# Masks added by VectorE with the maximum, and compressions' first layer in plain fp32 on four column groups

## The chip, the cores and the metric

One of the eight cores of a Trainium2 chip runs the kernel. The metric is the device time in microseconds, from the kernel's start to its end; lower is better.

## The reference

The kernel computes two transformer blocks over 256 tokens of width 1024, in fp32. The first has a gated feed-forward, a mixing stage (NSA attention with compressed, selected and windowed keys, next to sliding-window attention with sinks) and a second feed-forward. The second block has two layers, each with a mixing stage of three kinds (MLA, DSA with a top-k selection, retention) and a feed-forward. What the change touches is this:

```python
def _compress(kv, pe, w1, w2):                    # 15 blocks of 32 tokens, 2 groups
    blocks = jnp.concatenate([c[:, :-1], c[:, 1:]], axis=2)
    blocks = blocks + pe[None, None, :, None, :]
    flat = blocks.transpose(0, 1, 3, 2, 4).reshape(B, n_cmp, G, CMP_LEN * D)
    return jax.nn.gelu(flat @ w1) @ w2            # w1: 2048 x 256, w2: 256 x 64

s = jnp.einsum('bnqgrd,bnkgd->bngrqk', qb, kb) * (D ** -0.5)
s = jnp.where(mask[None, :, None, None], s, NEG_INF)
m = jnp.maximum(jnp.max(s, axis=-1, keepdims=True), sk)     # sk: the sinks, swa only
e = jnp.exp(s - m)
p = e / (jnp.sum(e, axis=-1, keepdims=True) + jnp.exp(sk - m))
```

Every attention (slc, win, swa in the first block, dsa and mla in the second) masks its scores, subtracts the row's maximum and takes the exponential. dsa's mask is computed at run time from the top-k selection, the others are constant.

## The kernel before

**Order.** One list, `schedule()` (L128), holds the steps of the whole program. Each engine walks the same list and issues its part of every step, so the list sets the order on every engine, and each engine works strictly in order. Semaphores join them.

**Weights.** Weights come in pieces ("slabs") of 1 MB, in a ring of three buffers `raw`. SP loads piece s when piece s - 3 no longer needs its buffer (L746). Precision is kept by splitting: ScalarE copies a piece to `w_hi` rounded (the high half, L998), VectorE writes the rest, raw minus high, to `w_lo` (the low half, L1357), and TensorE then makes three matmuls for each product: high times high, high times low, low times high (`group`, L1873). On ScalarE and VectorE `ahead` (L1005, L1365) issues the splits up to two pieces ahead of the step, before that step's own work. TensorE waits for the low half.

**Compressions.** Step `xpe` adds the position embeddings on VectorE (L1670, into `xpe`, 16 blocks of 30 columns), and both halves of the result are made (L1241, L1673). Step `cmp1` takes two pieces, of 8 blocks each: per block three matmuls with 30 stationary and 256 moving columns (L2149), all into one bank. ScalarE applies Gelu (L1247), TensorE turns the result (`cmpt`, L2158), ScalarE copies it, TensorE does the second layer (`cmp2`).

**Attention.** A "tile" is 128 queries: t = 0 has 128 keys, t = 1 has 256. Heads are handled in groups that fill one bank of 512 columns: four heads for t = 0, two for t = 1 (`groups`, L177; dsa has two in both). Two groups make a round: they sit on different halves of TensorE's rows, and their matmuls alternate (mla's groups stand alone). Per round:

- `s` on TensorE: a bf16 matmul of the identity with the mask starts the bank (L2199), then the plain fp32 score matmuls add to it (L2204). VectorE reduces the bank to the negative maximum of each head (L1687), ScalarE takes the exponential from the bank with that as bias, one head at a time, with the sum (L1285), and that frees the bank.
- `t`: TensorE turns the probabilities (L2212), VectorE copies them (L1702; dsa's ScalarE, L1294).
- `pv`: TensorE multiplies with the values (L2226).

In the first block nine rounds, slc 0, slc 1 (two), win 0, win 1 (two), swa 0, swa 1 (two), are interleaved with eight gate projections ("gate", one piece each, g0 to g7), so that a round's `t` comes one round after its `s`, and its `pv` one more after that. In the second block mla's and dsa's steps stand with fewer projections between them.

**Rope.** A projection is copied by ScalarE to `xs` (L1218), multiplied by a constant matrix on TensorE (L2138), and combined by VectorE in two passes (L1648, L1657), with a product from GpSimd (L972). A matmul in plain fp32 leaves two records in the trace.

## Time and profile before

| | |
|---|---|
| three runs, us | 1279.13, 1282.40, 1281.95; median 1281.95 |
| profiled execution, span | 1277.6 us (the time around its span isn't given) |
| TensorE busy | 1252.2 us (98%), 8858 matmul records |
| VectorE busy | 810.5 us (63%) |
| ScalarE busy | 613.4 us (48%) |
| GpSimd busy | 86.5 us (7%) |
| DMA | 209.94 MB, mean 164 GB/s |
| granted TensorE clock | full speed in all 40 slices |

The span is what the hardware profiler saw of one execution, from the first to the last instruction. A duration of a matmul contains the time that it takes to pass through the array, and overlaps the next one's: what a matmul costs is the distance from its start to the start of the next. PE is TensorE, PEld its weight loads, DVE VectorE, ACT ScalarE, POOL GpSimd, SP the engine that issues loads.

### The profile page before, as it was taken

The numbers are of one execution on the slowest core, as the hardware profiler recorded it, in microseconds if no ns is written. First come the engines' busy times: TensorE is split into PE (matmuls) and PEld (weight loads), VectorE is DVE, ScalarE is ACT, GpSimd is POOL, SyncE is SP. The second block draws the span as 40 slices with busy tenths as digits, with TensorE's granted clock in tenths as the row PEclk, the third lists the DMA queues.
The fourth block names the chain that finished last, engine by engine and source line by source line (L and its number), as shares of the span: only waits on it lengthen the run. The fifth ranks groups of instructions, "written<-read, shape, count | busy, mean of one in ns | idle before, by whom it ended". The sixth has DMA issues, their size and how long they took to land. (4 is left out here: it accounts for less than half of the span.)

```text
span 1277.6 us, 21605 instructions
## 1 busy us (share of the span) xinstructions
PE 1252.2 (98%) x8858; PEld 1151.6 (90%) x8858; DVE 810.5 (63%) x965; ACT 613.4 (48%) x836; POOL 86.5 (7%) x73
## 2 busy tenths in 40 slices
PE   8999999999999999999999999999999999999997
PEld 7999999989898999999998889999999978999996
DVE  5665556676866655556798756555459976655554
ACT  5443436473436443435744554444465364544443
POOL 0000001100000000001432000000014210000000
PEclk9999999999999999999999999999999999999999
DMA  9565666463236565556535056655644334565560
GB/s 284 191 208 195 195 161 165 156 199 101 98 108 206 178 194 188 190 175 187 166 108 165 16 179 201 196 177 187 189 134 149 91 131 148 166 197 175 187 197 33
DMA packets 181461, 209.94 MB, mean 164 GB/s; under 512 B 32537, under 2 KB 158097, under 8 KB 181265
## 3 DMA queue, kind: packets, MB, share of 16 engines
q1 hardware_dynamic: 180944, 208.52, 52.3%
q8 instruction: 49, 0.80, 0.3%
q10 hardware_dynamic: 448, 0.46, 0.1%
q14 instruction: 20, 0.16, 0.0%
HBM read 207.92 MB, written 1.05 MB: 164 GB/s over the span
## 5 line engine op out<-in xcount | busy, mean ns | idle before, releaser
L1357 DVE TENSOR_TENSOR w_lo<-raw,w_hi 128x2048 fp32r<-128x2048 f32 (+2 forms) x198 | 441.7, 2234 | 271.1 <-ACT w_hi L998 270.7
L998 ACT ACTIVATE w_hi<-raw 128x2048 fp32r<-128x2048 f32 (+2 forms) x198 | 367.8, 1861 | 234.6 <-PE bank L1879 215.6
L1879 PE MATMUL bank<-n_hi,w_hi 128*128 128x256 f32 (+1 forms) x1600 | 455.5, 285 | 1.2 <-DVE w_lo L1357 1.2
L1879 PE MATMUL bank<-n_hi,w_lo 128*128 128x256 f32 (+1 forms) x1600 | 452.5, 283 | 0.0
L1879 PE MATMUL bank<-n_lo,w_hi 128*128 128x256 f32 (+1 forms) x1600 | 452.5, 283 | 0.0
L1879 PEld LDWEIGHTS bank<-n_hi,w_hi 128*128 128x128 f32 (+1 forms) x1600 | 305.1, 191 | 5.1 <-DVE w_lo L1357 2.1
L1879 PEld LDWEIGHTS bank<-n_lo,w_hi 128*128 128x128 f32 (+1 forms) x1600 | 305.2, 191 | 2.3 <-issue 0.5
L1879 PEld LDWEIGHTS bank<-n_hi,w_lo 128*128 128x128 f32 (+1 forms) x1600 | 305.1, 191 | 0.0
L1879 PE MATMUL bank<-w_hi,hid_hi 128*128 128x512 f32 (+1 forms) x472 | 182.3, 386 | 1.3 <-DVE hid_lo L1430 1.1
L1879 PE MATMUL bank<-w_lo,hid_hi 128*128 128x512 f32 (+1 forms) x472 | 180.6, 383 | 0.0
L1879 PE MATMUL bank<-w_hi,hid_lo 128*128 128x512 f32 (+1 forms) x472 | 180.2, 382 | 0.0
L1879 PEld LDWEIGHTS bank<-w_hi,hid_hi 128*128 128x128 f32 (+1 forms) x472 | 86.2, 183 | 19.4 <-issue 2.5
L1879 PEld LDWEIGHTS bank<-w_hi,hid_lo 128*128 128x128 f32 (+1 forms) x472 | 86.0, 182 | 18.0
L1879 PEld LDWEIGHTS bank<-w_lo,hid_hi 128*128 128x128 f32 (+1 forms) x472 | 86.2, 183 | 16.1 <-issue 0.6
L1015 ACT ACTIVATE scr<-scr 128x512 f32<-128x512 f32 x22 | 13.9, 633 | 95.4 <-DVE scr L1412 95.4
L1879 PE MATMUL bank<-hid_hi,w_hi 128*96 128x256 f32 (+1 forms) x176 | 50.8, 289 | 2.4 <-issue 1.5
L1285 ACT ACTIVATE probs<-bank,negm 128x128 f32<-128x128 f32 (+1 forms) x96 | 39.0, 427 | 23.1 <-DVE negm L1687 23.1
L1879 PE MATMUL bank<-hid_lo,w_hi 128*96 128x256 f32 (+1 forms) x176 | 49.5, 281 | 0.0
L1879 PE MATMUL bank<-hid_hi,w_lo 128*96 128x256 f32 (+1 forms) x176 | 49.5, 281 | 0.0
L1426 DVE SCALAR_TENSOR_TENSOR scr<-bank,rstd 128x512 f32<-128x512 f32 x32 | 22.1, 691 | 42.2 <-PE bank L1879 42.1
L1956 PE MATMUL bank<-n_hi,w_hi 128*128 128x256 f32 x144 | 42.2, 293 | 3.3 <-DVE n_lo L1400 1.8
L1019 ACT ACTIVATE hid_hi<-scr 128x512 fp32r<-128x512 f32 x22 | 13.9, 630 | 59.2 <-DVE scr L1420 59.2
(259 smaller groups left out, 1527.6 us busy)
## 6 DMA issues: line engine op xcount, KB each, us to landing
raw<-in_w_ff_dram SPq DMA_DIRECT2D x64, 1024.0 KB, 5.3
raw<-in_w_in_dram SPq DMA_DIRECT2D x31, 1024.0 KB, 5.4
raw<-in_ffn_down_dram SPq DMA_DIRECT2D x22, 1024.0 KB, 5.0
raw<-in_ffn_up_dram SPq DMA_DIRECT2D x21, 1024.0 KB, 5.3
raw<-in_ffn_gate_dram SPq DMA_DIRECT2D x20, 1024.0 KB, 5.4
raw<-in_w_out_dram SPq DMA_DIRECT2D x12, 1024.0 KB, 5.2
raw<-in_w_uq_dram SPq DMA_DIRECT2D x8, 576.0 KB, 4.1
raw<-in_w_in_dram SPq DMA_DIRECT2D x12, 256.0 KB, 4.0
```

The costliest lines, as they stand in the source:

```text
L998: nc.scalar.activation(w_hi[:, s % SPLIT, c0:n], raw[:, s % RING, c0:n], ACT.Copy).then_inc(hi_ready, 1)
L1015: nc.scalar.activation(silu_sb, silu_sb, ACT.Silu).then_inc(silu_ready, 1)
L1019: nc.scalar.activation(hid_hi[:, buf, :], hid[:, buf, :], ACT.Copy).then_inc(hidh_ready, 1)
L1285: last = nc.scalar.activation(probs[:, buf, c], pb[:, c], ACT.Exp, bias=negm[:, buf, i:i + 1], accum_out=rsum[:, RSLOT[a], t, h:h + 1])
L1357: V.tensor_tensor(w_lo[:, s % SPLIT, c0:n], raw[:, s % RING, c0:n], w_hi[:, s % SPLIT, c0:n].bitcast(f32), ALU.subtract).then_inc(lo_ready, 1)
L1426: V.scalar_tensor_tensor(halves(silu_sb), halves(bank[b][:, :]), 0.0, r2(), ALU.max, ALU.mult).then_inc(bank_free[b], 1)
L1879: mm = MM(out, stat(k, a), mov(k, b), start=(first and k == 0 and n == 0), stop=(last and k == K - 1 and n == 2), skip_group_check=True)
L1956: mm = MM(pb[:, m * T:m * T + T], w(s, a)[:, k * T + m * P:k * T + m * P + P], xn(k, b), start=(k == 0 and m == 0 and j == 0), stop=(k == ...
```

## The change

Three parts.

1. **Masks.** The mask matmuls go. VectorE's step `s` becomes, for each head, one `tensor_tensor_reduce`: it adds score and mask, negates, writes the result to `probs` in SBUF and reduces it to the minimum (the negative maximum). Each is two instructions, the pass and a read of the accumulator. VectorE's last pass frees the bank, ScalarE's exponential reads `probs` with scale -1 and writes it in place. Since VectorE now writes `probs`, it is VectorE that waits for the transposes of four groups before.
2. **Compressions.** The four pieces of `cmp1` (k and v, two halves each) are not split; TensorE reads `raw`. Per block one plain fp32 matmul, 32 stationary columns (`xpe` is padded), block i to the column group i mod 4, which is partitions 32(i mod 4) and on of the bank. Step `cmpt` is a matmul with a constant `fold` that turns and adds the four groups in one; Gelu moves behind it. The buffer of such a piece is free when TensorE has multiplied it (`slab_done`), where it was when VectorE had split it.
3. **Order.** In `schedule()` slc 1 comes before slc 0 (its first round needs only the rope of nq0), cmp1 of k stands before the first scores, projection sq1 and the rope of nq1 between the first and the second round of scores, cmp1 of v after gate 1.

```diff
@@ schedule @@
           ("rope", 0, "nq0"), ("proj", 0, "vv"), ("rope", 0, "sk"), ("proj", 0, "sq0"), ("rope", 0, "k"),
-          ("xpe", "k"), ("proj", 0, "nq1"), ("rope", 0, "sq0"), ("xpe", "v"), ("proj", 0, "sq1")]
-    scores, turned, weighted = in_rounds(0, [(a, t) for a in ("slc", "win", "swa") for t in range(NT)])
+          ("xpe", "k"), ("proj", 0, "nq1"), ("rope", 0, "sq0"), ("xpe", "v"), ("cmp1", "k")]
+    scores, turned, weighted = in_rounds(0, [("slc", 1), ("slc", 0)] + [(a, t) for a in ("win", "swa") for t in range(NT)])
-    S += [("rope", 0, "nq1"), ("cmp1", "k")] + scores[0] + [("rope", 0, "sq1"), ("cmp1", "v")] + scores[1] + turned[0]
-    S += gate[0] + [("cmpt", "k")] + scores[2] + weighted[0] + turned[1]
-    S += gate[1] + [("cmp2", "k"), ("cmpt", "v")] + scores[3] + weighted[1] + turned[2]
-    S += gate[2] + [("cmp2", "v"), ("rope", 0, "kc")] + scores[4] + weighted[2] + turned[3]
-    S += gate[3] + [("cs", 0)] + scores[5] + weighted[3] + turned[4]
+    S += scores[0] + [("proj", 0, "sq1"), ("rope", 0, "nq1"), ("cmpt", "k")] + scores[1] + [("rope", 0, "sq1")] + turned[0]
+    S += gate[0] + [("cmp2", "k")] + scores[2] + weighted[0] + turned[1]
+    S += gate[1] + [("cmp1", "v"), ("rope", 0, "kc")] + scores[3] + weighted[1] + turned[2]
+    S += gate[2] + [("cmpt", "v")] + scores[4] + weighted[2] + turned[3]
+    S += gate[3] + [("cmp2", "v"), ("cs", 0)] + scores[5] + weighted[3] + turned[4]
@@ load_slab @@
-            if s >= RING:
-                sp.wait_ge(lo_ready, s - RING + 1)
+            if s >= RING and slabs[s - RING][0] == "cmp1":
+                sp.wait_ge(slab_done, s - RING + 1)
+            elif s >= RING:
+                sp.wait_ge(lo_ready, LOC[s - RING])
@@ ScalarE @@
                 elif kind == "cmp1":
                     ahead(SL[st + (0,)])
                     ahead(SL[st + (1,)])
                     pb = await_bank(act, st)
-                    nc.scalar.activation(cmp_h[:, v, :], pb[0:2 * NCMP, 0:T], ACT.Gelu_apprx_tanh).then_inc(freed(st), 1)
+                    nc.scalar.activation(cmp_h[:, v, :], pb[:, 0:T], ACT.Copy).then_inc(freed(st), 1)
...
-                    act.wait_ge(negm_ready, q + 1)
-                    if q >= 4:
-                        await_bank(act, ("t",) + ATTLIST[q - 4])
+                    act.wait_ge(*free_count(st))
...
-                        last = nc.scalar.activation(probs[:, buf, c], pb[:, c], ACT.Exp, bias=negm[:, buf, i:i + 1],
+                        last = nc.scalar.activation(probs[:, buf, c], probs[:, buf, c], ACT.Exp, bias=negm[:, buf, i:i + 1], scale=-1.0,
                                                     accum_out=rsum[:, RSLOT[a], t, h:h + 1])
-                    last.then_inc(freed(st), 1)
+                    last.then_inc(exp_done, 1)
@@ VectorE @@
-                    ins = V.tensor_reduce(negm[:, buf, 0:nh], pb[:, 0:nh * nk].rearrange("p (h k) -> p h k", h=nh), AX.X, ALU.max, negate=True)
+                    if q >= 4:
+                        await_bank(dve, ("t",) + ATTLIST[q - 4])
+                    if a == "dsa":
+                        dve.wait_ge(retv_done, l)
+                        dve.wait_ge(sel_ready, 2 * (l - 1) + t + 1)
+                    for i in range(nh):
+                        c = slice(i * nk, i * nk + nk)
+                        ins = V.tensor_tensor_reduce(out=probs[:, buf, c], in0=pb[:, c], in1=mask_of(a, t), scale=-1.0, scalar=3e38,
+                                                     op0=ALU.add, op1=ALU.min, accum_out=negm[:, buf, i:i + 1])
+                    ins.then_inc(freed(st), 1)
@@ TensorE @@
-                    pe.wait_ge(xpel_ready, v + 1)
+                    pe.wait_ge(xpe_ready, v + 1)
                     for half in range(2):
                         s = SL[st + (half,)]
-                        weights(s)
+                        pe.wait_ge(raw_ready[s % RING], RAWC[s])
                         for i in range(8):
-                            c = (8 * half + i) * 30
-                            mm = group(pb[0:2 * NCMP, 0:256], 1, lambda k, lo: (xpe_lo if lo else xpe_hi)[:, v, c:c + 30],
-                                       lambda k, lo: w(s, lo)[:, i * 256:i * 256 + 256], first=(half == 0 and i == 0),
-                                       last=(half == 1 and i == 7))
+                            r = slice(32 * (i % 4), 32 * (i % 4) + 32)
+                            mm = MM(pb[r, 0:256], xpe[v][:, 256 * half + 32 * i:256 * half + 32 * i + 32], raw[:, s % RING, i * 256:i * 256 + 256],
+                                    start=(half == 0 and i < 4), stop=(half == 1 and i >= 4), skip_group_check=True)
                         mm.then_inc(slab_done, 1)
...
-                        mm = nc.tensor.transpose(pb[:, m * P:m * P + 2 * NCMP], cmp_h[:, v, m * P:m * P + P], ident[0:2 * NCMP, 0:2 * NCMP])
+                        mm = MM(pb[:, m * P:m * P + 32], cmp_h[:, v, m * P:m * P + P], con("fold"), start=True, stop=True, skip_group_check=True)
...
-                    for pb, heads, _ in sides:
-                        nh = len(heads)
-                        part = pb[:, 0:nh * nk].rearrange("p (h k) -> p h k", h=nh)
-                        m = mask_of(a, t)
-                        if a in ("slc", "win", "mla"):
-                            part, m = part[:, :, t * P:t * P + P], m[:, t * P:t * P + P]
-                        MM(part, identb[:, :], m.unsqueeze(1).to_broadcast([P, nh, m.shape[1]]), start=True, stop=False, skip_group_check=True)
```

**Where instructions move.** First VectorE between the rope of k and that of nq1. `work` is the compressions' input, `turn_s` and the `scr` beside it are a rope's two passes, `w_lo` a low half, `negm` the negative maxima. Before (the rope of nq1 is the pair in the middle):

```order
L1670 TENSOR_TENSOR work<-work,gains 128x8x15 x3
L1673 TENSOR_TENSOR hid_lo<-work,hid_hi 128x480 [waits xpeh_ready]
L1357 TENSOR_TENSOR w_lo<-raw,w_hi 128x2048 [waits hi_ready]
L1648 TENSOR_TENSOR turn_s<-bank,rvt 128x512 [waits rope_done,tab_ready,bank_ready1]
L1657 TENSOR_TENSOR scr<-turn_c,turn_s 128x512 [waits turnc_ready,bank_free1]
L1357 TENSOR_TENSOR w_lo<-raw,w_hi 128x2048 [waits hi_ready] x2
L1687 TENSOR_REDUCE negm<-bank 128x4 [waits bank_ready7]
L1687 TENSOR_REDUCE negm<-bank 128x4 [waits bank_ready4]
```

After the change (the rope of sq0, the v blocks, the low halves of sq1 and g0, the first round, the low half of g1, the rope of nq1):

```order
L1652 TENSOR_TENSOR turn_s<-bank,rvt 128x512 [waits rope_done,tab_ready,bank_ready0]
L1661 TENSOR_TENSOR scr<-turn_c,turn_s 128x512 [waits turnc_ready,bank_free0]
L1671 MEMSET work 128x32 [waits xpe_ready]
L1675 TENSOR_TENSOR work<-work,gains 128x8x15 x4
L1361 TENSOR_TENSOR w_lo<-raw,w_hi 128x2048 [waits hi_ready] x2
L1697 ISA probs,negm<-bank,masks 128x256 [waits bank_ready6]
L1697 ISA negm 128x1
...
L1361 TENSOR_TENSOR w_lo<-raw,w_hi 128x2048 [waits hi_ready]
L1652 TENSOR_TENSOR turn_s<-bank,rvt 128x512 [waits rope_done,tab_ready,bank_ready5]
L1661 TENSOR_TENSOR scr<-turn_c,turn_s 128x512 [waits turnc_ready,bank_free5]
```

The rope of nq1, which stood ahead of the first maxima, now stands behind the first round and behind the low half of g1.

Second ScalarE around the compression of k: `w_hi` is a high half, `xs` a projection's copy. Before:

```order
L1218 ACTIVATE xs<-bank 128x512 [waits slab_done,rope_done]
L998 ACTIVATE w_hi<-raw 128x2048 [waits slab_done,raw_ready1]
L998 ACTIVATE w_hi<-raw 128x2048 [waits slab_done,raw_ready2]
L1247 ACT_TABLE_LOAD
L1247 ACTIVATE rgt<-bank 30x256 [waits slab_done]
L1285 ACT_TABLE_LOAD
L1285 ACTIVATE probs,rsum<-bank,negm 128x128 [waits negm_ready]
```

Now (the high halves are those of sq1, g0 and g1; the last `xs` is sq1's):

```order
L1228 ACTIVATE xs<-bank 128x512 [waits slab_done,rope_done] x2
L1008 ACTIVATE w_hi<-raw 128x2048 [waits slab_done,raw_ready0]
L1008 ACTIVATE w_hi<-raw 128x2048 [waits slab_done,raw_ready1]
L1253 ACTIVATE rgt<-bank 128x256 [waits slab_done]
L1287 ACT_TABLE_LOAD
L1287 ACTIVATE probs,rsum<-probs,negm 128x256 [waits bank_free6]
...
L1008 ACTIVATE w_hi<-raw 128x2048 [waits slab_done,raw_ready2]
L1228 ACTIVATE xs<-bank 128x512 [waits slab_done,rope_done]
```

The high half of g1 and the copy of sq1 now stand behind the first round's exponentials.

Third ScalarE around the compression of v. Before, with the high halves of two gate pieces ahead of Gelu:

```order
L998 ACTIVATE w_hi<-raw 128x2048 [waits slab_done,raw_ready0]
L998 ACTIVATE w_hi<-raw 128x2048 [waits slab_done,raw_ready1]
L1247 ACT_TABLE_LOAD
L1247 ACTIVATE rgt<-bank 30x256 [waits slab_done]
L1285 ACT_TABLE_LOAD
```

Now, with those of g2 and g3 ahead of the copy that frees the compression's bank:

```order
L1287 ACTIVATE probs,rsum<-probs,negm 128x128 [waits bank_free5]
L1287 ACTIVATE probs,rsum<-probs,negm 128x128 x3
L1008 ACTIVATE w_hi<-raw 128x2048 [waits slab_done,raw_ready2]
L1008 ACTIVATE w_hi<-raw 128x2048 [waits slab_done,raw_ready0]
L1253 ACTIVATE rgt<-bank 128x256 [waits slab_done]
```

g3 shares its `raw` buffer with the first half of v, and so its load waits for TensorE there.

## Rows read from the trace of the kernel before

**Rows 1.** The page's first part: busy time, share, instructions.

```profile
PE 1252.2 (98%) x8858; PEld 1151.6 (90%) x8858; DVE 810.5 (63%) x965; ACT 613.4 (48%) x836; POOL 86.5 (7%) x73
```

**Rows 2.** Windows: stretch, length, busy us of each engine (instructions), clock, DMA, GB/s.

```profile
247.05:357.64 110.59, 110.02 (x915) 100.39 (x913) 82.55 (x127) 61.28 (x144) 5.45 (x3) 1.00 0.43 134
695.40:711.00 15.60, 12.96 (x84) 10.13 (x83) 14.37 (x24) 12.29 (x27) 3.10 (x2) 1.00 0.18 68
```

**Rows 3.** TensorE's timeline, 246 to 261 us: start, us, engine, line, operation, count.

```profile
246.59 1.02 PE L2138 MATMUL bank<-xs,cst 128*128 128x512 f32 x2
247.05 0.68 PE L1879 MATMUL bank<-n_hi,w_hi 128*128 128x256 f32 x1
...
253.66 0.68 PE L1879 MATMUL bank<-w_hi,hid_hi 128*30 128x256 f32 x1
...
259.60 0.60 PE L2199 MATMUL bank<-masks,identb 128*128 128x512 bf16 x2
260.13 1.16 PE L2204 MATMUL bank<-scr 64*128 64x128 f32 x16
```

**Rows 4.** TensorE's timeline at the second round of scores.

```profile
267.73 0.39 PE L2199 MATMUL bank<-masks,identb 128*128 128x256 bf16 x2
268.06 1.13 PE L2204 MATMUL bank<-scr 64*128 64x256 f32 x8
```

**Rows 5.** The mask matmuls' line, and TensorE's timeline at mla's first scores.

```profile
L2199 PE MATMUL bank<-masks,identb x30: 269/283/389, 259.6 to 1056.6; 128*128 128x256 bf16 x16, 128*128 128x512 bf16 x14
L2199 PE MATMUL bank<-selb,identb x8: 273/330/377, 694.4 to 1033.7; 128*128 128x256 bf16 x4, 128*128 128x512 bf16 x4
...
709.53 0.38 PE L2199 MATMUL bank<-masks,identb 128*128 128x512 bf16 x1
709.75 1.06 PE L2204 MATMUL bank<-scr 96*128 96x128 f32 x8
...
711.75 0.28 PE L2199 MATMUL bank<-masks,identb 128*128 128x256 bf16 x1
711.87 1.03 PE L2204 MATMUL bank<-scr 96*128 96x256 f32 x4
712.73 0.27 PE L2199 MATMUL bank<-masks,identb 128*128 128x256 bf16 x1
```

**Rows 6.** TensorE's timeline: index scores on four row groups.

```profile
641.92 1.15 PE L2260 MATMUL bank<-scr 32*128 32x256 f32 x16
642.99 0.38 PE L1879 MATMUL bank<-n_hi,w_hi 128*128 128x256 f32 x1
```

**Rows 7.** The page's groups for the low and the high half; a load's landing.

```profile
L1357 DVE TENSOR_TENSOR w_lo<-raw,w_hi 128x2048 fp32r<-128x2048 f32 (+2 forms) x198 | 441.7, 2234 | 271.1 <-ACT w_hi L998 270.7
L998 ACT ACTIVATE w_hi<-raw 128x2048 fp32r<-128x2048 f32 (+2 forms) x198 | 367.8, 1861 | 234.6 <-PE bank L1879 215.6
...
DMA to landing us min/median/max: 3.9/5.2/10.6
```

**Rows 8.** VectorE's and ScalarE's timelines, 250 to 274 us.

```profile
250.26 1.17 DVE L1670 TENSOR_TENSOR work<-work,gains 128x120 f32<-128x120 f32 x4
...
262.23 1.28 DVE L1687 TENSOR_REDUCE negm<-bank 128x4 f32<-128x512 f32 x2
...
272.82 0.47 ACT L1285 ACTIVATE probs<-bank,negm 128x256 f32<-128x256 f32 x1 [0.38 <-DVE negm L1687]
273.19 0.19 ACT L1285 ACTIVATION_READ_ACCUMULATOR probs<-bank,negm 128x1 f32 x1
273.29 0.47 ACT L1285 ACTIVATE probs<-bank,negm 128x256 f32<-128x256 f32 x1
```

**Rows 9.** Timelines in the second block's first layer: dsa's and mla's first reductions, TensorE's longest wait.

```profile
695.49 0.76 DVE L1687 TENSOR_REDUCE negm<-bank 128x2 f32<-128x256 f32 x2 [0.32 <-PE bank L2204]
...
703.26 1.07 PE L2138 MATMUL bank<-xs,cst 96*96 96x512 f32 x2 [2.18 <-ACT probs L1285]
...
710.84 0.69 DVE L1687 TENSOR_REDUCE negm<-bank 128x4 f32<-128x512 f32 x1 [0.44 <-PE bank L2204]
```

More of the change, by code:

```diff
@@ L102, in constants @@
     put("blk", (rows[:, None] // CP == np.arange(8)[None, :]).astype(np.float32))
+    put("fold", (rows[:, None] % 32 == np.arange(32)[None, :]).astype(np.float32))
     q, k = np.arange(P)[:, None], np.arange(P)[None, :]
@@ L332, in two_blocks @@
         x2 = wflat[:, 0:1024].rearrange("p (v g t) -> p v g t", v=2, g=2)[:, :, :, :]
-        xpe = wflat[:, 1024:1024 + 480]
+        xpe = [wflat[:, at:at + 512] for at in (1024, 0)]
         vblk = wflat[:, 1536:2048]
@@ L620, in two_blocks @@
         ATTLIST = sorted(ATT, key=ATT.get)
+        SINKS = {st: n + 1 for n, st in enumerate(st for st in ATTLIST if st[1] == "swa")}
         IDX = [(t, [j, j + 4]) for t in range(NT) for j in range(4)]
@@ L1273, in _ @@
                     buf = q % 4
-                    act.wait_ge(negm_ready, q + 1)
-                    if q >= 4:
-                        await_bank(act, ("t",) + ATTLIST[q - 4])
-                    if a == "dsa":
-                        act.wait_ge(retv_done, l)
-                    pb = bank[JOB[st][0]]
+                    act.wait_ge(*free_count(st))
                     if a == "swa":
+                        act.wait_ge(sink_seen, SINKS[st[1:]])
                         hs = slice(heads[0], heads[-1] + 1, 2)
@@ L1669, in _ @@
                             src = x2[:, v, g, 16 * a:16 * a + 240].rearrange("p (c b e) -> p b c e", b=8, e=2)[:, :, :, 0]
-                            last = V.tensor_tensor(out_v[:, a, :, g, :], src, bc(gains[:, pe0 + 8 * a:pe0 + 8 * a + 8], 8, NCMP), ALU.add)
+                            last = V.tensor_tensor(out_v[:, a, :, g, 0:NCMP], src, bc(gains[:, pe0 + 8 * a:pe0 + 8 * a + 8], 8, NCMP), ALU.add)
                     last.then_inc(xpe_ready, 1)
-                    dve.wait_ge(xpeh_ready, v + 1)
-                    V.tensor_tensor(xpe_lo[:, v, :], xpe, xpe_hi[:, v, :].bitcast(f32), ALU.subtract).then_inc(xpel_ready, 1)
                 elif kind == "cmp1":
@@ L2187, in _ @@
                             pe.wait_ge(*free_count(("ukv", l, 1)))
-                        if a == "dsa":
-                            pe.wait_ge(sel_ready, 2 * (l - 1) + t + 1)
                     if a == "mla":
```

66 lines of the change are left out of this document (36 added, 30 removed).

## The prediction

> **What bounds the kernel now.** I read the page first: TensorE is busy 1252.2 of 1277.6 us [rows 1]. Then the windows: in the stretch that the change reorders, 247.05 to 357.64 us, TensorE is busy 110.02 of 110.59 us at a granted clock of 1.00, while VectorE is busy 82.55 and ScalarE 61.28 [rows 2]. So there every matmul removed is worth its time, unless the shortened work uncovers a wait. Third, the timeline for the price of each piece. A matmul's duration overlaps the next one's, so prices are differences of starts. Last, VectorE's timeline in the second block, where it is busy 14.37 of 15.60 us [rows 2]: there it has no room for new work. The profiled execution's own time is not given; its span of 1277.6 lies 4.35 us under the median of the three runs, 1281.95, so I forecast a difference and add it to the median.
>
> **Masks, on TensorE.** 38 mask matmuls go [rows 5]. In the first block a pair over 512 columns costs 260.13 - 259.60 = 0.53 us [rows 3], one over 256 columns 268.06 - 267.73 = 0.33 [rows 4]. There are five wide pairs (slc 0, win 0, swa 0 and both rounds of swa 1) and four narrow ones (both rounds of slc 1 and of win 1): 2.65 + 4 x 0.31 to 0.33, so 3.9. In each layer of the second block: a narrow and a wide pair for dsa (0.85), two wide single ones at 0.22 and four narrow ones at 0.12 for mla (0.92) [rows 5], 1.75 together.
>
> **Compressions' first layer.** Each takes 48 matmuls from 253.66 to 259.60, 5.94 us [rows 3]. Now it is 16 plain fp32 ones with 256 moving columns. A plain one of that shape costs (712.73 - 711.87) / 2 = 0.43 us: in mla four records, two matmuls, stood in 0.86 (the record at 711.87 runs 1.03 with its tail) [rows 5]. One after the other, 16 cost 6.9. Eight such matmuls on four row groups took 642.99 - 641.92 = 1.07 us [rows 6], two deep instead of eight: 0.87 and 0.2 for filling. No row shows column groups. If they overlap as row groups do, four deep is 1.74 + 0.2 = 1.94; ends 1.7 and 6.9, and I take 1.94, since the nearest row is idx. Saved: 2 x 4.0 = 8.0. The Trainium skill (TensorE: Matmul & The Clock Gate, section "Why this matters for your kernels") has column groups within a few ns of row groups, at 2.38x for three tiles; by that ratio a compression would take 2.9 us. Fold, memset and the wider constants cost under 0.2 us and lie beside other work.
>
> **VectorE's new price.** A group's maximum was one reduction, 0.60 us apart (two in 1.28) [rows 8]. Now each head has a masked minimum and a separate read of the accumulator: 96 of each. The split of 2048 columns takes 2.23, which is (2.23 - 0.68) / 1536 = 1.0 ns a column beyond the reduction's 512 [rows 7, 8]; so 0.60 is 0.52 of streaming and 0.08 of overhead, and a pass over 256 columns lies between 0.34 (pipelined) and 0.42 (its whole duration, 0.68 less 0.26). The read lies between 0 and the 0.19 that ScalarE's takes [rows 8]. I take 0.45 a head, close to the pipelined end, as reductions are pipelined; ends 0.34 and 0.61. For 128 columns: 0.32, ends 0.21 and 0.48. Four heads of 256 take 1.8 instead of 1.2, eight of 128 take 2.6.
>
> **Waits uncovered in the first block.** The short compression no longer covers the weights' pipeline. I take a load as 5.2 us to landing, ScalarE's high half as 1.9 and VectorE's low half as 2.2 us [rows 7]. By hand, from 247.05, where the compression of k now starts:
> 1. It ends at 249.0, the first scores at 250.1. The next projection, sq1, needs its low half, and VectorE has that behind rope sq0 (starts about 247.7, two passes, to 249.4) and the v blocks (four adds, 1.17 [rows 8], and a memset, to 250.8): ready 253.1. **TensorE waits 3.0.** It projects until 259.3 (6.15: 6.61 from 247.05 to 253.66 less a rope's 0.46 [rows 3]), then rope nq1 and the fold, to 260.3.
> 2. Gate piece g0 can be loaded only when the first half of k is multiplied, 248.2: landed 253.5, high 255.4, low 257.7. Only then come the masked minima (259.4), ScalarE's exponentials (0.45 apart [rows 8], to 260.4), the high half of g1 (262.3), its low half (264.6), and behind that on VectorE rope nq1, two passes (266.0). The second round of scores needs rope nq1: **TensorE waits 5.7.** No transposes stand between to fill it.
> 3. The same at v. There ScalarE's split of g3 stands ahead of the copy that frees the compression's bank, and gate 2 wants that bank. g3 is loaded after half of v: 5.2 + 1.9 + 0.4 + 0.1 of semaphores = 7.6 us; TensorE has 4.8 of other work (the second half, rope kc, scores, values, transposes). **2.8.** ScalarE is late by that for the next exponentials and g4, and gate 3's bank is freed behind g4's low half: **1.3.**
> Sum 12.8 of waits against 3.9 + 8.0 = 11.9 saved: +0.9 us. Later rounds keep VectorE under the round: the fullest has about 9.5 us of work and gains 0.6, against 10.5.
>
> **Second block.** VectorE is in one chain from 695.49 to the first mla reduction at 710.84 [rows 9], with only 0.44 of idle at its end. dsa's heads add 0.5 + 0.6, less 0.32 because its scores end earlier: first mla minimum about 0.3 us later and 0.6 longer. TensorE, 1.75 ahead, and 1.3 more from the wait of 2.18 before rope uq2 [rows 9] (bank 4 is now freed by VectorE, not by the exponentials), then stands at the scores of mla's second group, whose rope uq3 is in that chain. The rest of mla follows the exponentials. I find the end of mla 0.3 us later than before, in each layer: the masks' 1.75 is lost there. Ends of the price: 0.3 earlier, and 2.5 later. Total: 0.9 + 2 x 0.3 = **+1.5 us**, 1283.5.
>
> **Rivals.**
> - *The saving holds more than I find.* If the minima cost the pipelined end, and loads land a microsecond sooner (once at k, once at v), the waits lose 2 to 3 us, and where the second block's chain has slack its masks' 3.5 are kept: 0.9 - 2.5 - 3.5 = -5, 1277. For: VectorE idles 0.44 before mla. Against: it is a single in-order queue, and three costs must err the same way.
> - *The clock falls in the new wait.* Before, TensorE idles at most 2.18 us at once behind the start [rows 9], and the granted clock is 1.00 [rows 2]; the new wait of 5.7 has no like there. At 1.2 GHz, the scores, rope and transposes behind it (2.4 us) and part of a gate projection of 5.84 cost as much again: about +3, so 1286.5. It decides once a wait is long enough, which no row shows. The Trainium skill (TensorE: Matmul & The Clock Gate, "What's actually happening") says the array falls to half its clock when idle and needs sustained work to rise; by that rule the gap would be charged.
> - *The minima are dear.* At 0.61 and 0.48 the second block ends 2.5 later per layer and the k wait is 0.6 longer: +6, 1288. It decides from about 0.5 a head. For: two instructions per head; against: reductions overlap.
> - *The groups don't run together*, so that this part doesn't do what it says: 6.9 instead of 1.94 each. Of the 5.0 added at k half is absorbed (waits 1 shrinks), and so at v: first halves end 2.5 later, +5, so 1288.5. Against: row groups overlap [rows 6].
>
> **How the numbers follow.** About 0.3% (3.8 us) is what a measurement can tell from no change. Forecast 0.40 (its own range 1279 to 1286), first rival 0.25, clock 0.17, dear minima 0.10, serial groups 0.08. Faster takes 0.20 of the first rival and 0.05 of the forecast's lower edge; slower takes the last three (0.35 less the mild half of the clock's, 0.05) and 0.05 of the upper edge; the rest, 0.40, is the same. The range that leaves out two in ten is 1275 to 1290: from the first rival with a further 2 us to the serial case and its bounds.
>
> **What would show it.** Right: two gaps on TensorE near 250 to 253 and 260 to 266, released by the low half of sq1 and by VectorE's rope nq1; one of 2 to 3 us before gate 2, released by ScalarE's copy; compressions of 2 us; in 695 to 726 a VectorE without idle time and an end of mla at the same distance from its start as before. Wrong: a dense TensorE between 247 and 350 (then the change is worth some 10 us), compressions of 6 us or more, a granted clock under 1 behind 266, or a masked minimum of half a microsecond or more.

## The result, and the profile after

| kernel | median of 8 runs, us | ratio to the kernel before, 95% interval |
|---|---|---|
| before | 1281.38 (1279.13 to 1282.40) | |
| the change | 1284.88 (1283.74 to 1285.88) | 1.0031 [1.0021, 1.0042] |

The change makes the kernel slower by 3.5 us: measurable, and at the edge of the 0.3% that the prediction had taken as the least that can be told. The span of the profiled execution went from 1277.6 to 1282.2, 4.6 us more. That is more than the medians say because the profiled execution of the kernel before is one of its shortest: an execution of it with a span of 1277.5 took 1279.3, 2.1 under the median, and the change's profiled one took 1284.29, 0.6 under its own. The page's first part, beside [rows 1]:

```profile
PE 1242.6 (97%) x8792; PEld 1142.6 (89%) x8792; DVE 804.9 (63%) x1115; ACT 609.0 (48%) x831; POOL 85.6 (7%) x73
```

TensorE is busy 9.6 us less than before, and the span is 4.6 us longer: 14 us of new idle time. The page can't say where it lies. The windows can, where those of [rows 2] stood. The first mixing stage is now 116.62 us long, with a granted clock of 0.97. This window begins with the rotation of sq0, which stood just ahead of that of [rows 2]; counted from there too (246.59), the stage took 111.05 before, so it is 5.6 longer.

```profile
247.00:363.62 116.62, 102.83 (x870) 93.08 (x869) 77.96 (x202) 60.42 (x142) 4.46 (x3) 0.97 0.43 136
```

So in this stage TensorE idles 13.8 us. Its waits there (line waited for and what released it; total, times, longest):

```profile
PE bank L2207 <- DVE scr L1661: 7.2, 1, 7.2
PE bank L1890 <- ACT rgt L1253: 2.9, 1, 2.9
PE bank L1890 <- DVE w_lo L1361: 2.2, 1, 2.2
PE bank L1890 <- DVE scr L1630: 1.2, 1, 1.2
```

A fifth is 0.2, 13.7 in all. Before, the same stage had 0.6 us of waits, both short ones before scores. TensorE's timeline at the first two waits, beside [rows 3, 4]:

```profile
247.00 1.02 PE L2149 MATMUL bank<-xs,cst 128*128 128x512 f32 x2
247.95 1.93 PE L2160 MATMUL bank<-raw,work 128*32 128x256 f32 x32
249.81 1.13 PE L2207 MATMUL bank<-scr 64*128 64x256 f32 x8
253.11 0.39 PE L1890 MATMUL bank<-n_hi,w_hi 128*128 128x256 f32 x1 [2.16 <-DVE w_lo L1361]
...
259.83 0.54 PE L2168 MATMUL bank<-cst,rgt 128*128 128x32 f32 x4
267.58 2.08 PE L2207 MATMUL bank<-scr 64*128 64x256 f32 x8 [7.21 <-DVE scr L1661]
269.59 2.07 PE L2149 MATMUL bank<-xs,cst 128*128 128x512 f32 x2
271.46 1.35 PE L2215 MATMUL bank<-cst,probs 128*128 128x128 f32 x8
272.56 0.36 PE L1890 MATMUL bank<-n_hi,w_hi 128*128 128x256 f32 x1
```

The compression takes 1.86 us (247.95 to 249.81): the column groups do run together. Then come both gaps that the prediction named. What TensorE waits for in the second is VectorE's rotation of nq1, and VectorE's timeline shows what stands ahead of it:

```profile
250.78 2.27 DVE L1361 TENSOR_TENSOR w_lo<-raw,w_hi 128x2048 fp32r<-128x2048 f32 x1
256.64 2.29 DVE L1361 TENSOR_TENSOR w_lo<-raw,w_hi 128x2048 fp32r<-128x2048 f32 x1 [3.59 <-ACT w_hi L1008]
258.85 0.42 DVE L1697 CUSTOM_DVE_ANT_0 probs<-bank,masks 128x256 f32<-128x256 f32 x1
259.19 0.08 DVE L1697 DVE_READ_ACCUMULATOR2_ANT negm<- 128x1 f32 x1
259.19 0.42 DVE L1697 CUSTOM_DVE_ANT_0 probs<-bank,masks 128x256 f32<-128x256 f32 x1
...
263.56 2.29 DVE L1361 TENSOR_TENSOR w_lo<-raw,w_hi 128x2048 fp32r<-128x2048 f32 x1 [3.25 <-ACT w_hi L1008]
265.77 0.68 DVE L1652 TENSOR_TENSOR turn_s<-bank,rvt 128x512 f32<-128x512 f32 x1
266.49 1.04 DVE L1661 TENSOR_TENSOR scr<-turn_c,turn_s 128x512 f32<-128x512 f32 x1
```

The low halves at 256.64 and 263.56 are g0's and g1's. Each waits for ScalarE's high half. That of g0 waits for a load, that of g1 for the exponentials between:

```profile
254.69 1.92 ACT L1008 ACTIVATE w_hi<-raw 128x2048 fp32r<-128x2048 f32 x1 [5.04 <-DMA raw<-in_w_in_dram]
...
259.66 0.51 ACT L1287 ACTIVATE probs<-probs,negm 128x256 f32<-128x256 f32 x1 [1.48 <-DVE negm L1697]
...
261.64 1.89 ACT L1008 ACTIVATE w_hi<-raw 128x2048 fp32r<-128x2048 f32 x1
```

And TensorE's granted clock around the long wait, in windows of one to two us (busy, clock, DMA share, GB/s):

```profile
262.00:264.00 2.00, 0.00 (x0) 1.00 0.89 312
264.00:266.00 2.00, 0.00 (x0) 0.81 0.00 0
266.00:267.00 1.00, 0.00 (x0) 0.50 0.14 13
267.00:268.00 1.00, 0.42 (x2) 0.50 0.83 164
...
271.00:272.00 1.00, 1.00 (x4) 0.50 0.00 0
272.00:273.00 1.00, 1.00 (x11) 0.96 0.00 0
```

It falls to the lower level, 1.2 GHz, in a wait of 7.2 us, and stays there until 272. The scores and the rotation behind the wait take 3.88 us to the transposes (267.58 to 271.46), and it is 4.98 to gate 0, at 272.56. So the mechanism of the rival "the clock falls in the new wait" was there as well.

How late each later point of the program is, from the first starts of each layer's output projection (line 2346 before):

| start, us | before | change | masks alone | both, old order |
|---|---|---|---|---|
| output projection, first block | 382.88 | 388.85 (+6.0) | 381.57 (-1.3) | 380.23 (-2.7) |
| second block, layer 1 | 727.45 | 733.12 (+5.7) | 725.83 (-1.6) | 724.50 (-3.0) |
| second block, layer 2 | 1065.50 | 1070.23 (+4.7) | 1063.54 (-2.0) | 1062.25 (-3.3) |

Of the 6.0 us, 0.4 are there when the first mixing stage begins and 5.6 arise in it. The second block gives back 1.2.

### The profile page after: what moved, and what is told of

Same layout as the page of the kernel before. It is cut to its first block and busy times, and to the rows that moved or that the text cites. A ratio compares the mean times of both kernels' runs of the same rounds, so it can differ in the third digit from the quotient of the medians.

```text
span 1282.2 us, 21620 instructions
## 1 busy us (share of the span) xinstructions
PE 1242.6 (97%) x8792; PEld 1142.6 (89%) x8792; DVE 804.9 (63%) x1115; ACT 609.0 (48%) x831; POOL 85.6 (7%) x73
## 5 line engine op out<-in xcount | busy, mean ns | idle before, releaser
L1361 DVE TENSOR_TENSOR w_lo<-raw,w_hi 128x2048 fp32r<-128x2048 f32 (+2 forms) x194 | 432.7, 2233 | 275.9 <-ACT w_hi L1008 275.5
L1008 ACT ACTIVATE w_hi<-raw 128x2048 fp32r<-128x2048 f32 (+2 forms) x194 | 359.9, 1859 | 248.4 <-PE bank L1890 214.8
L1890 PE MATMUL bank<-w_hi,hid_hi 128*128 128x512 f32 x440 | 173.0, 393 | 1.3 <-DVE hid_lo L1434 1.1
L1890 PE MATMUL bank<-w_lo,hid_hi 128*128 128x512 f32 x440 | 171.8, 390 | 0.0
L1890 PE MATMUL bank<-w_hi,hid_lo 128*128 128x512 f32 x440 | 171.3, 389 | 0.0
L1890 PEld LDWEIGHTS bank<-w_hi,hid_hi 128*128 128x128 f32 x440 | 82.8, 188 | 18.5 <-issue 2.0
L1890 PEld LDWEIGHTS bank<-w_hi,hid_lo 128*128 128x128 f32 x440 | 82.6, 188 | 17.5
L1890 PEld LDWEIGHTS bank<-w_lo,hid_hi 128*128 128x128 f32 x440 | 82.8, 188 | 15.4
L1287 ACT ACTIVATE probs<-probs,negm 128x256 f32<-128x256 f32 (+1 forms) x96 | 42.4, 442 | 22.0 <-DVE negm L1697 22.0
L1434 DVE TENSOR_TENSOR hid_lo<-scr,hid_hi 128x512 fp32r<-128x512 f32 x54 | 37.0, 685 | 8.0 <-ACT hid_hi L1036 4.9
```

Of the source, the lines that this page charges most:

```text
L1008: nc.scalar.activation(wh(s)[:, c0:n], raw[:, s % RING, c0:n], ACT.Copy).then_inc(hi_ready, 1)
L1287: last = nc.scalar.activation(probs[:, buf, c], probs[:, buf, c], ACT.Exp, bias=negm[:, buf, i:i + 1], scale=-1.0, accum_out=rsum[:, RSLOT ...
L1361: V.tensor_tensor(wl(s)[:, c0:n], raw[:, s % RING, c0:n], wh(s)[:, c0:n].bitcast(f32), ALU.subtract).then_inc(lo_ready, 1)
L1434: V.tensor_tensor(hid_lo[:, buf, :], hid[:, buf, :], hid_hi[:, buf, :].bitcast(f32), ALU.subtract).then_inc(hidl_ready, 1)
L1890: mm = MM(out, stat(k, a), mov(k, b), start=(first and k == 0 and n == 0), stop=(last and k == K - 1 and n == 2), skip_group_check=True)
```

## The experiments

All ratios are to the kernel before, run beside them; its medians lie between 1280.5 and 1281.4. Where two kernels that didn't run beside each other are compared below, it is by medians, and the ratios give the same within 0.8 us. Theory: the loss is made by the waits that the short compressions uncover in the new order. Rivals: VectorE's masked minima make it; or any order pays it.

**First group: the change taken apart.** Three parts can be set independently: masks on VectorE, short compressions, the new order.

| kernel | masks | compressions | order | median, us | ratio [95%] |
|---|---|---|---|---|---|
| masks_only | new | old | old | 1277.51 | 0.9981 [0.9971, 0.9991] |
| comp_only | old | new | old | 1280.74 | 1.0006 [0.9995, 1.0018] |
| both_old_order | new | new | old | 1277.16 | 0.9975 [0.9964, 0.9987] |
| comp_order | old | new | new | 1288.57 | 1.0061 [1.0047, 1.0075] |
| the change | new | new | new | 1284.88 | 1.0031 [1.0021, 1.0042] |

masks_only, against the kernel before:

```diff
-                        MM(part, identb[:, :], m.unsqueeze(1).to_broadcast([P, nh, m.shape[1]]), start=True, stop=False, skip_group_check=True)
+                        ins = V.tensor_tensor_reduce(out=probs[:, buf, c], in0=pb[:, c], in1=mask_of(a, t), scale=-1.0, scalar=3e38,
+                                                     op0=ALU.add, op1=ALU.min, accum_out=negm[:, buf, i:i + 1])
```

> Only the masks are moved to VectorE; the compressions and the order are those of the kernel before. Theory (the loss is made by the short compressions in the new order, not by the masked minima): the first block ends 3 to 4 us sooner, since the long compressions still cover the weights, and the second block about 1.4 us sooner, as in the change; 1276 to 1278 against 1281.4, with no wait of TensorE over 2.5 us between 247 and 358. Rival (the minima themselves fill VectorE's queue and cost what the masks save): 1281 to 1284.

The theory holds: no wait over 1.0 us in the stage. But the first block gains 1.3 where 3 to 4 were expected, and the second 0.7 where 1.4 were. In the first, new waits take 1.6 (2.2 instead of 0.6). Most of the rest is a price that was read wrongly. TensorE's timeline of this kernel at the place of [rows 3, 4]:

```profile
259.75 0.28 PE L1884 MATMUL bank<-w_hi,hid_lo 128*30 128x256 f32 x1
259.96 1.16 PE L2200 MATMUL bank<-scr 64*128 64x128 f32 x16
...
267.44 0.28 PE L1884 MATMUL bank<-w_hi,hid_lo 128*30 128x256 f32 x1
267.64 1.13 PE L2200 MATMUL bank<-scr 64*128 64x256 f32 x8
```

Scores now follow the last split product after 0.20 to 0.21 us, where the mask matmul had followed it after 0.12 (259.48 to 259.60). The scores now pay 0.09 that the mask matmul had not, so a wide pair is worth 0.53 - 0.09 = 0.44, a narrow one 0.24: 5 x 0.44 + 4 x 0.24 = 3.2, not 3.9.

comp_only:

```diff
-                            mm = group(pb[0:2 * NCMP, 0:256], 1, lambda k, lo: (xpe_lo if lo else xpe_hi)[:, v, c:c + 30],
-                                       lambda k, lo: w(s, lo)[:, i * 256:i * 256 + 256], first=(half == 0 and i == 0),
-                                       last=(half == 1 and i == 7))
+                            mm = MM(pb[r, 0:256], xpe[v][:, 256 * half + 32 * i:256 * half + 32 * i + 32], raw[:, s % RING, i * 256:i * 256 + 256],
+                                    start=(half == 0 and i < 4), stop=(half == 1 and i >= 4), skip_group_check=True)
```

> Only the compressions are changed (plain fp32 on four column groups); masks stay on TensorE and the order is that of the kernel before. Theory: 8 us of matmuls go, and waits for the weights of the gates take most of it back, because a gate's piece is loaded only when a compression's piece is multiplied, which is as much sooner as the compression is shorter only for the piece behind it: 1277 to 1280. Rival (the new order is needed for the short compression): 1283 or more, with a wait as long as 7 us.

No difference from before can be measured: 8 us of matmuls are gone and all of it is given back. The trace has a wait of 4.3 us for gate 0's low half and a clock of 0.71 and 0.60 in the two windows of five us from 265 to 275. 1280.74 is 0.7 over the theory's range, and the wait is 3 us short of the rival's: the theory had the mechanism and was optimistic.

both_old_order, against the change (the lines of the schedule from there to the compressions' ends as before):

```diff
-          ("xpe", "k"), ("proj", 0, "nq1"), ("rope", 0, "sq0"), ("xpe", "v"), ("cmp1", "k")]
+          ("xpe", "k"), ("proj", 0, "nq1"), ("rope", 0, "sq0"), ("xpe", "v"), ("proj", 0, "sq1")]
...
-    S += scores[0] + [("proj", 0, "sq1"), ("rope", 0, "nq1"), ("cmpt", "k")] + scores[1] + [("rope", 0, "sq1")] + turned[0]
+    S += [("rope", 0, "nq1"), ("cmp1", "k")] + scores[0] + [("rope", 0, "sq1"), ("cmp1", "v")] + scores[1] + turned[0]
```

> Masks and compressions as in the change, the order of the first mixing stage as before. Theory (the order is what loses, since the second scores there stand behind a rotation that VectorE does after two halves of weights): 1273 to 1278, faster than both. Rival (any order pays the wait, because the short compression uncovers the weights): within 1 us of the change, 1284 to 1286.

Both parts of arithmetic with the old order beat the kernel before: **the reordering is what loses**, 7.7 us between this kernel and the change. "Any order pays" falls, though this order pays too. Its two longest waits in the stage:

```profile
PE bank L1890 <- DVE w_lo L1361: 4.1, 1, 4.1
PE bank L2160 <- DMA raw<-in_cmp_v_w_dram: 1.6, 1, 1.6
```

comp_order keeps the change and puts the mask matmuls of the kernel before back:

```diff
+                        MM(part, identb[:, :], m.unsqueeze(1).to_broadcast([P, nh, m.shape[1]]), start=True, stop=False, skip_group_check=True)
-                        ins = V.tensor_tensor_reduce(out=probs[:, buf, c], in0=pb[:, c], in1=mask_of(a, t), scale=-1.0, scalar=3e38,
-                                                     op0=ALU.add, op1=ALU.min, accum_out=negm[:, buf, i:i + 1])
```

> The compressions and the order of the change, masks still on TensorE. Theory: the long wait before the second scores stays, 6 to 7 us, only 1.2 shorter for the cheaper maxima, and TensorE has 5.3 us of masks more: 1286 to 1289. Rival (the minima make the long wait): 1282 or less, the wait under 4 us.

In the new order the masks on VectorE gain 3.7 us. The wait before the second scores is 5.5 without the minima (6 to 7 were expected), 7.2 with them: they lengthen it, they don't make it.

**Second group: the waits, one at a time, in the change.**

rope_first:

```diff
-    S += scores[0] + [("proj", 0, "sq1"), ("rope", 0, "nq1"), ("cmpt", "k")] + scores[1] + [("rope", 0, "sq1")] + turned[0]
+    S += scores[0] + [("rope", 0, "nq1"), ("proj", 0, "sq1"), ("cmpt", "k")] + scores[1] + [("rope", 0, "sq1")] + turned[0]
```

> The change with one step moved: the rotation of nq1 is issued ahead of the projection sq1, on TensorE and in VectorE's queue, so that VectorE does it before the low half of g1. Theory (the second scores wait for that rotation behind g1's two halves, and the clock falls in the wait): the wait of 7.2 us goes but for about 1 us at the next transposes, and the matmuls behind it run at full clock (2.2 us more): 1276 to 1279 against 1284.9 of the change. Rival (the exponentials and the loads bound this place anyway): the wait moves to the transposes or to gate 0 and keeps 5 us or more, 1282 to 1285.

1279.92, ratio 0.9995 [0.9987, 1.0004]: 5.0 us better than the change, between the two expectations. The wait before the second scores went, and another came, at a place neither had seen:

```profile
PE bank L1890 <- ACT rgt L1253: 8.0, 2, 5.0
```

Banks are handed out in turn. With the rotation moved up, sq1 gets the compression's bank, and ScalarE frees that only behind g0's high half (256.12; the copy follows at 257.94). In this wait too the granted clock falls, to 0.50 from 258 to 264. The other of the two, 2.9, is the wait before gate 2, unchanged.

copy_first:

```diff
-                    ahead(SL[st + (1,)])
+                    ahead(SL[st + (1,)], 1)
                     pb = await_bank(act, st)
                     nc.scalar.activation(cmp_h[:, v, :], pb[:, 0:T], ACT.Copy).then_inc(freed(st), 1)
+                    ahead(SL[st + (1,)])
```

> The change with ScalarE's copy of the compression's sums put ahead of the split of the piece after next (g0 at k, g3 at v). Theory (gate 2 waits for the bank that this copy frees): the wait of 2.9 us near 295 goes and nothing takes its place but part of the 1.2 behind it: 1281.5 to 1283. Rival (the low half of g2 or the exponentials are as late): the wait stays over 2 us under another name, 1284 to 1285.

1285.25, 1.0031 [1.0020, 1.0042]: nothing gained, the rival is right. Gate 2 no longer waits, and two waits behind it took its place, 1.27 before scores and one before gate 3:

```profile
308.81 0.47 PE L1891 MATMUL bank<-n_hi,w_hi 128*128 128x256 f32 x1 [2.61 <-DVE scr L1631]
```

ScalarE shows why. The copy moved from 297.08 to 290.15, but g3's high half starts at 295.01 instead of 295.27, still behind its load, and with it everything that both queues hold behind g3:

```profile
290.15 0.38 ACT L1253 ACTIVATE rgt<-bank 128x256 f32<-128x256 f32 x1 [4.49 <-PE bank L2161]
295.01 1.92 ACT L1008 ACTIVATE w_hi<-raw 128x2048 fp32r<-128x2048 f32 x1 [4.48 <-DMA raw<-in_w_in_dram]
```

rope_copy has both diffs.

> Both of these edits in the change. Theory (two separate waits, so the gains add): 1273 to 1276.5, faster than the kernel before by 4 us or more and than the change in the old order. Rival (the second wait was a consequence of the first): as with the rotation alone, 1277 to 1279.

1280.26, 0.9998 [0.9989, 1.0007]. The gains don't add. The waits of 5.0 and 2.9 us are gone, and seven small ones of 0.5 to 2.6 stand in their place, 8.5 us in all; the clock falls to 0.50 among them (266 to 268).

busy_gap asks what the fallen clock is worth (`keep_busy` multiplies zeros into a bank that is not in use there):

```diff
                     elif g == 0 or st[2:] == ("slc", 1, 2):
+                        if st[2:] == ("slc", 1, 2):
+                            keep_busy(32)
```

> The change with 32 matmuls of zeros over 512 columns, into a bank that nobody uses there, put between the fold of k and the second scores, where TensorE waits 7.2 us: the wait is the same, TensorE only isn't idle in it. Theory (the clock falls because it idles, and that costs what runs at the low level behind it, 267.6 to 272): granted clock 1.00 from 260 to 275, the gates after it 2 to 2.5 us earlier, 1282 to 1283. Rival (the fallen clock costs nothing, since the matmuls behind the gap are bound by something else): 1284.5 or more.

1283.04, 1.0015 [1.0007, 1.0024], 1.8 us better than the change with the same gap in the work:

```profile
261.33 7.07 PE L2006 MATMUL bank<-zerob 128*128 128x512 bf16 x32
268.33 1.14 PE L2214 MATMUL bank<-scr 64*128 64x256 f32 x8
269.40 1.12 PE L2154 MATMUL bank<-xs,cst 128*128 128x512 f32 x2
270.36 1.04 PE L2222 MATMUL bank<-cst,probs 128*128 128x128 f32 x8
271.15 0.36 PE L1890 MATMUL bank<-n_hi,w_hi 128*128 128x256 f32 x1
```

The clock is 1.00 from 258 on. From the scores to the transposes it is 2.03 us instead of 3.88, and to gate 0 it is 2.82 instead of 4.98: in the trace the fallen clock costs 2.2 us. The rival falls. The medians show 1.8 and the spans only 0.9. One reason is in this trace: VectorE ends the rotation at 267.65, 0.12 later than in the change, but the zeros run on until 268.33. The fold ahead of them came 1.1 later than in the change (260.97 against 259.83), since in this execution the first wait had cost the clock too, for 2.15 us of idleness against 2.16 in the change (windows of busy_gap):

```profile
252.00:253.00 1.00, 0.23 (x2) 1.00 1.06 379
253.00:254.00 1.00, 1.00 (x9) 0.80 1.08 377
254.00:255.00 1.00, 1.00 (x6) 0.50 1.11 357
...
257.00:258.00 1.00, 1.00 (x10) 0.99 1.10 351
```

In the change's own profile it stayed at 1.00 there.

**Third group: what makes the softmax late.** After copy_first the theory had to be restated: a split whose load is late holds up the minima and exponentials behind it in two in-order queues. Two conditions, so two ways out. One takes the late split out of the softmax's way. The second argument of `ahead` is how many pieces beyond the step's own are split (late_splits):

```diff
@@ the change with the rotation moved as in rope_first, then ScalarE, at a compression: the copy comes before the split of the piece after next @@
-                    ahead(SL[st + (0,)])
-                    ahead(SL[st + (1,)])
+                    ahead(SL[st + (0,)], 1)
+                    ahead(SL[st + (1,)], 1)
@@ VectorE, at a compression @@
-                    ahead(SL[st + (0,)])
-                    ahead(SL[st + (1,)])
+                    ahead(SL[st + (1,)], 1)
@@ both engines @@
                 elif kind == "gate":
-                    ahead(SL[st])
+                    ahead(SL[st], 1 if st[1] == 2 else 2)
```

> Rotation of nq1 first, ScalarE's copy of the compression's sums first, and on both engines only the next piece of weights is split at a compression and at gate 2 (g0 comes behind the first minima and exponentials, g3 behind those of gate 2's round). Theory (what stays in the kernel with the two edits is softmax work queued behind a split whose load is late): the waits near 261 to 266 and 299 to 307 go, the clock stays: 1272 to 1276. Rival (the loads themselves are late, so each wait moves to the weights): 1278 to 1281.

late_splits2 has also, on both engines:

```diff
-                    ahead(SL[st])
+                    ahead(SL[st], 1 if st == ("proj", 0, "sq1") else 2)
```

> The same, and at the projection sq1 only g0 is split, so g1 comes behind the second round's minima. Theory: the transposes of the first round are no later and the second round's softmax is earlier, within 1 us of the kernel with late splits alone, 1272 to 1276. Rival (loads are late): 1278 to 1281.

1268.98, 0.9906 [0.9888, 0.9924], and 1268.78, 0.9905 [0.9887, 0.9923]: **12 us faster than the kernel before**, 3 to 7 beyond what was expected. The only wait of TensorE in the stage that the list shows is 1.1 us, and the clock is 1.00. VectorE's and TensorE's rows of late_splits2 at the place of the long wait:

```profile
252.52 0.41 DVE L1696 CUSTOM_DVE_ANT_0 probs<-bank,masks 128x256 f32<-128x256 f32 x1
...
257.24 2.29 DVE L1361 TENSOR_TENSOR w_lo<-raw,w_hi 128x2048 fp32r<-128x2048 f32 x1 [1.93 <-ACT w_hi L1008]
```

```profile
252.66 0.39 PE L1889 MATMUL bank<-n_hi,w_hi 128*128 128x256 f32 x1 [1.10 <-DVE w_lo L1361]
...
258.52 0.53 PE L2167 MATMUL bank<-cst,rgt 128*128 128x32 f32 x4
258.97 1.14 PE L2206 MATMUL bank<-scr 64*128 64x256 f32 x8
```

The first minimum comes at 252.52, ahead of g0's low half, not at 258.85 behind it. The load of g0 is as late as in the change: it is issued 1.13 us after the compression's start in both (247.50 and 248.63 here, 247.95 and 249.08 there).

The other way out makes the loads early. In the change the compressions' pieces are multiplied from the ring of three loads itself and hold their places there until then; before, a split freed the place. The DMA view of the change, 240 to 300 us in 40 slices of 1.5 us, has long holes, from 240 to 249 and, but for single packets, from 272 to 289:

```profile
DMA  0000003899999598008920000000000002899999
GB/s 0 0 0 0 0 0 23 236 386 356 344 345 359 144 325 289 0 9 210 378 102 0 0 0 0 0 0 16 0 5 0 0 0 18 224 382 363 347 349 347
```

copied, against rope_copy, lets ScalarE copy such a piece, and TensorE multiply the copy, which leaves out the low-order bits of these weights:

```diff
-            if s >= RING and slabs[s - RING][0] == "cmp1":
-                sp.wait_ge(slab_done, s - RING + 1)
-            elif s >= RING:
+            if s >= RING:
...
+                if slabs[s][0] == "cmp1":
+                    nc.scalar.activation(wh(s)[:, :], raw[:, s % RING, :], ACT.Copy).then_inc(hi_ready, 1)
+                    return
```

> Rotation and copy first, as in the kernel with the two edits (1280.3), and ScalarE copies each of the four pieces of compression weights into the buffer of the high halves, so that its place in the ring of three loads is free at the copy, as it was in the kernel before, and not at the multiplication. The high halves alone are multiplied, so this leaves out the low-order bits of these weights. Theory (the pieces that wait in the ring to be multiplied stop the loads; the DMAs stand idle from 244 to 249 and 272 to 289): g0 and g3 land 4 us or more sooner, the waits near 262 and 300 go though ScalarE has 7.6 us more to do: 1273 to 1277. Rival (the order of VectorE's queue alone makes these waits): 1280 or more.

1269.75, 0.9910 [0.9895, 0.9926], 3 us beyond what was expected. The rival (VectorE's order alone) falls: with rope_copy's queues unchanged, earlier loads are worth 10.5 us, and that with 7.6 us more of work on ScalarE.

copied_alone has the same edit on the change itself.

> The change in its own order and with its own queues, and only the four pieces of compression weights copied by ScalarE so that their places in the ring are free early (high halves alone multiplied, so the low-order bits of these weights are left out). Theory (the late loads and the rotation behind the split are two conditions of one wait, and either edit alone shortens it): g0 is split from 250 on, the first minima come about 3.5 us earlier, but the rotation of nq1 still stands behind g1's two halves, which follow the exponentials: a wait of about 3.5 to 4 us before the second scores in place of 7.2, less lost to the clock, and none over 2 us behind 290: 1274 to 1279. Rival A (the loads alone made the waits): within 1 us of the kernel that has both edits too, 1269 to 1271. Rival B (VectorE's queue alone): 1283 to 1285.

1275.36, 0.9958 [0.9945, 0.9972], within the theory's range and outside both rivals'. The wait before the second scores:

```profile
PE bank L2205 <- DVE scr L1659: 2.1, 1, 2.1
```

2.1 us instead of 7.2, shorter than the 3.5 expected; the rotation still stands behind g1's low half (260.84). The two conditions are shown: early loads alone give 9.5 us, and the two small reorderings on top 5.6 more. Both ways out together (late splits and early loads) were not run.

## Why the prediction was right, and where it was wrong

The median, 1284.88, is 1.4 us over the forecast of 1283.5. As a difference the forecast was +1.5 and the result is +3.5, or +4.6 by the spans. That is nearer to the clock rival than to the forecast, and the steps show why. They show also that the nearness of the total is in part luck: the first mixing stage was forecast at +0.9 and found at +5.6, and the second block, forecast at +0.6 and found at -1.2, gave part of the miss back.

- **Waits: right in place, cause and order; nearly right in size.** Forecast 3.0, 5.7, 2.8 and 1.3, together 12.8; found 2.2, 7.2, 2.9 and 1.2, together 13.5. The first is short because TensorE came to it late: sq1's low half was ready at 253.1 as forecast, but the scores before it began at 249.8 and not 249.0. The second is long because the load of g0 was issued at 249.08 and landed by 254.69, not 248.2 and 253.5:

```profile
249.08 1.23 SPq L796 DMA_DIRECT2D raw<-in_w_in_dram  x2
```

  Of the 0.9 in the issue, 0.4 is that all before 247 was that much later, and 0.5 that the rotation of sq0, now ahead of the plain fp32 compression, takes 0.95 and not 0.46 [rows 3]. The load itself took 5.6 and not 5.3. The delay of 1.2 passed undiminished down the chain, with 0.3 more added on the way, to the rotation, ready at 267.5 and not 266.0. The case behind that number, two queues in order with one late load at the head, was right. The 0.6 of waits that the stage had before was not taken off.
- **The clock: the step that failed.** The forecast charged nothing for it and gave the rival 0.17. It was known that a wait of 5.7 had no like in the trace; the waits of up to 2.2 us in [rows 9] said nothing of one that long. It fell to 0.50, and the stretch behind the wait took 2.2 us longer than in busy_gap at 1.00 (the rival had said 3); in some executions it falls after the first wait too, which neither had. The Trainium skill (TensorE: Matmul & The Clock Gate, "What's actually happening") has the array fall to half its clock when idle: this trace agrees, with 0.50.
- **Masks: 3.9 was 3.2.** The price came from the mask's own start to the scores' start, and left out that the scores then pay 0.09 that the mask had not.
- **Compressions: 8.0 was 8.15, and what stands beside them costs 1.8.** One took 1.86 us against the forecast of 1.94, the best-founded guess by its outcome: 16 matmuls at 0.43 are 6.9, so four column groups ran 3.7 times as fast. The Trainium skill (same page, "Why this matters for your kernels") gives 2.38 for three tiles; by that ratio it would have been 2.9, and this case with four is faster. The prediction took each rotation of a projection at 0.46 and the fold at under 0.2, beside other work. But the three rotations of the stage stand ahead of plain fp32 matmuls now and cost 1.3 more on TensorE at full clock, and the two folds 1.00 where the two transposes before took 0.53.
- **VectorE's price: too high, on the safe side.** Taken as 0.45 a head of 256 columns and 0.32 of 128; found 0.345 and 0.21, the pipelined ends of both ranges. The separate read takes 0.08 and is hidden.
- **Second block: wrong sign.** Forecast 0.3 later per layer, found 0.4 earlier in each: in layer 1 its first scores step starts 6.08 late (694.42 and 700.50) and the output projection 5.67, in layer 2 5.16 (1032.47 and 1037.63) and 4.73. The end named for a cheap minimum was 0.3 earlier. VectorE's chain bound it, as said: the first mla minimum is at 716.89, just 6.05 behind that of [rows 9]; of the masks' 1.75 little is kept. Another 0.5 came between the layers, about as much as one wait shrank that the list calls "issue" (1.1 us before, 0.5 after); its cause stays open.

The first stage can be added up from the distances between TensorE's starts in both profiles. Waits grew by 13.2 (0.6 to 13.8). The masks' matmuls took 3.9 and are gone, the compressions' went from 11.9 to 3.7. Against these 12.1 stand 2.2 for the clock, 1.3 for the rotations, 0.5 for the folds and 0.4 in small shares elsewhere, among them what the scores pay now that no mask matmul stands before them. That gives +5.6, which is what the stage is longer. So of the 4.7 us that the forecast of this stage missed, the clock is about half, the rotations and folds 1.8, and the waits 0.4.

What the prediction didn't look for is the way out. It took the loads' lateness as given by the short compression. The ring of three, whose places the unsplit pieces now hold, was read in the code and priced only as a load that starts late; that its lateness passes on only through the queues' order was there to be read too, and it was worth 16 us between the change and late_splits2.

## What to carry to other kernels

When a change makes a covering piece of work shorter, follow each load, split and small vector step that it covered through every in-order queue, by hand; here that gave four waits within 0.1 to 1.5 us of the truth. Then ask of each whether what stands behind the late step needs it: moving the softmax ahead of a split that waits for a load turned 0.3% slower into 0.95% faster, with the same work and g0's load as late as in the change. And remove the wait that the next one hides behind too: one fix gave nothing, another 5 us, two together no more than one, and all of them 16.

## What the runs showed of the hardware that was not expected

- A wait of 7.2 us took TensorE's granted clock from 1.00 to 0.81 and 0.50, and it stayed at 0.50 for the first 4.4 us of work. Behind waits of 5.0 (rope_first), 4.3 (comp_only) and 4.1 (both_old_order) it was at 0.50 as well. A wait of 2.2 us before sq1 left it at 1.00 in the profile of the change and took it to 0.50 for two to three us in those of busy_gap, copy_first and copied_alone, behind the same work. In rope_copy no wait from 260 to 266 was over 1.3 us, but 3.3 of these 6 us were idle, and the clock was 0.81 and 0.50 from 264 to 268. What decides between these cases the traces do not tell.
- Four column groups of 32 columns, plain fp32, 16 matmuls of 256 moving columns each: 1.86 us, 3.7 times as fast as one after the other at the 0.43 of [rows 5].
- A masked minimum with its result written out: 0.345 us a head of 256 columns read from PSUM, 0.21 of 128; the read of its accumulator 0.08, hidden.
- ScalarE's exponentials of 256 columns stand 0.49 apart reading SBUF, and stood 0.47 apart reading PSUM [rows 8].
- The first plain fp32 matmul behind a group of split products costs 0.09 us more than a bf16 one there, and a rotation of 512 columns takes 0.86 to 0.96 ahead of plain fp32 matmuls (247.00, 258.97, and 269.40 in busy_gap), 0.46 ahead of split products [rows 3].
